# Differential attention with both maps' scores on row halves of the array, and a reordered neighbourhood attention

## What is computed

```python
def diff_attention(q, k, v, lam):            # q (B,Sq,H,2,d): 4 heads, two maps of d = 64
    s = einsum('bqhmd,bkhmd->bhmqk', qb, k) * scale
    p = softmax(s, axis=-1)
    a = p[:, :, 0] - lam * p[:, :, 1]
    return einsum('bhqk,bkhe->bqhe', a, v)
# latent queries: 512 own keys (with rotary) and 128 cached keys; prompt queries: 128 own keys
y_diff = rms_norm(y_diff, subln_g) * (1 - lam_init)

# neighbourhood attention, 8 heads of 64: softmax over an 8 x 16 window of the grid
# (with a relative bias) and the 128 cached keys; prompt queries: plain softmax
```

## Time and profile before

| | us |
|---|---|
| runs before | 2065.28, 2064.86, 2063.15 (median 2064.86) |
| the profiled execution's own time | 2058.49 |
| its span in the trace | 2056.4 |
| PE busy | 1963.3 (95% of the span) |
| DVE busy | 955.7 (46%) |
| ACT busy | 647.1 (31%) |
| POOL busy | 593.6 (29%) |
| differential stages | 236 to 456 and 1248 to 1451 |
| neighbourhood stages | 478 to 712 and 1473 to 1706 |

### The profile page before, as it was taken

How to read it: one execution, slowest core, us unless ns; L and a number is a source line. 1 busy time by engine, 2 the same in 40 slices (tenths; PEclk the granted TensorE clock), 3 DMA queues, 4 the chain that set the end, 5 groups by cost and what they waited for, 6 DMA issues and landing times.

```text
span 2056.4 us, 30590 instructions
## 1 busy us (share of the span) xinstructions
PE 1963.3 (95%) x12384; PEld 1782.0 (87%) x12384; DVE 955.7 (46%) x1480; ACT 647.1 (31%) x1101; POOL 593.6 (29%) x278
## 2 busy tenths in 40 slices
PE   6799989999999999999999999999999999999998
PEld 3698877889898999999878988888988899999996
DVE  5798666453444463421352143445344555443022
ACT  4323233323343321221352233333243332223121
POOL 2434311213222232233333332222322223313331
PEclk9999999999999999999999999999999999999999
DMA  7444320112121131122322221111221113212231
GB/s 294 151 158 145 127 101 31 42 52 93 61 64 52 62 102 62 52 72 81 125 101 94 88 72 62 42 42 42 83 72 62 57 58 99 66 51 72 72 111 74
DMA packets 50955, 172.13 MB, mean 84 GB/s; under 512 B 6656, under 2 KB 7296, under 8 KB 50816
## 3 DMA queue, kind: packets, MB, share of 16 engines
q1 hardware_dynamic: 41024, 146.60, 21.0%
q10 hardware_dynamic: 9792, 23.58, 3.3%
HBM read 162.82 MB, written 7.34 MB: 83 GB/s over the span
## 4 chain that ended last, share of the span: by engine, by line
PE 78%; DVE 14%; issue 4%; ACT 2%; DMA 1%; POOL 0%; SPq 0%; ACTq 0%; DVEq 0%; POOLq 0%
PE ps L1614 53%; PE ps L1502 4%; PE ps L1504 4%; PE ps L1503 4%; DVE mixed L1057 4%; PE ps L1688 3%; PE ps L1707 2%; PE ps L1726 1%; PE ps L1716 1%; DVE Pm L1328 1%; DVE nmax L1286 1%; ACT Pm L977 1%; DMA stage<-in_w_mod 1%; PE ps L1679 1%; PE ps L1689 1%
## 5 line engine op out<-in xcount | busy, mean ns | idle before, releaser
L728 POOL TENSOR_TENSOR wlo<-raw,whi 128x1024 fp32r<-128x1024 f32 x224 | 563.3, 2515 | 1319.7 <-ACT whi L786 1317.6
L1614 PE MATMUL ps<-bufB,whi 128*128 128x320 f32 x2816 | 541.8, 315 | 6.5 <-DVE vn L1183 4.0
L1614 PE MATMUL ps<-bufA,whi 128*128 128x320 f32 x2816 | 540.7, 314 | 4.9 <-DVE z L1448 1.4
L1614 PEld LDWEIGHTS ps<-bufB,whi 128*128 128x128 f32 x2816 | 443.5, 190 | 16.5 <-issue 11.5
L1614 PEld LDWEIGHTS ps<-bufA,whi 128*128 128x128 f32 x2816 | 442.3, 189 | 14.9 <-issue 10.1
L1614 PE MATMUL ps<-bufB,wlo 128*128 128x320 f32 x1408 | 323.4, 311 | 0.0
L1614 PE MATMUL ps<-bufA,wlo 128*128 128x320 f32 x1408 | 323.2, 311 | 0.0
L786 ACT ACTIVATE whi<-raw 128x1024 fp32r<-128x1024 f32 x224 | 237.6, 1061 | 210.5 <-PE ps L1614 125.0
L1614 PEld LDWEIGHTS ps<-bufB,wlo 128*128 128x128 f32 x1408 | 237.7, 190 | 0.0
L1614 PEld LDWEIGHTS ps<-bufA,wlo 128*128 128x128 f32 x1408 | 237.5, 189 | 0.0
L977 ACT ACTIVATE Pm<-ps,nmax 128x640 f32<-128x640 f32 (+2 forms) x160 | 100.0, 625 | 364.8 <-DVE nmax L1286 339.7
(11 more groups left out here) (217 smaller groups left out, 1898.6 us busy)
## 6 DMA issues: line engine op xcount, KB each, us to landing
raw<-in_wstream SPq DMA_DIRECT2D x224, 512.0 KB, 3.3
stage<-in_wstream SPq DMA_DIRECT2D x32, 512.0 KB, 4.5
stage<-in_w_mod SPq DMA_DIRECT2D x16, 512.0 KB, 15.2
out_y_sample<-X ACTq DMA_DIRECT2D x8, 512.0 KB, 2.7
Pm<-in_rpb ACTq DMA_DIRECT2D x12, 256.0 KB, 2.8
X<-in_x_sample SPq DMA_DIRECT2D x4, 512.0 KB, 10.9
xres<-in_x_sample ACTq DMA_DIRECT2D x4, 512.0 KB, 5.8
xres<-out_y_sample ACTq DMA_DIRECT2D x4, 512.0 KB, 5.9
```

The source lines that it names most:

```text
L728: pool.tensor_tensor(wlo[:, s % SPLITS, :], raw[:, s % RAWS, :], whi[:, s % SPLITS, :].bitcast(F32), ALU.subtract).then_inc(sems["lo"], 1)
L1614: ins = pe.matmul(ps[:, 2 * b + n, 0:HALF], wt[:, cols], src[:, part, base + k, n * HALF:(n + 1) * HALF], start=k == 0 and wt is hi and pa ...
```

## The change

In the differential stage one `S` step now makes both maps. The 512 own keys go in two halves of 256; for each half, map 0 is multiplied on rows 0 to 63 and map 1 on rows 64 to 127, into banks 4 and 5. The 128 cached keys of both maps go to a free quarter of banks 6 and 7, behind a wait for the copy and the value eviction of earlier units; ACT copies them to `Pm` at once. DVE takes the maximum of both maps' own keys in one instruction, of the cached keys in a second, and the smaller of the negated maxima in a third. A new step `EX` holds the exponentials: two for own keys, then two for cached keys (in place in `Pm`, with sums in `ectx`). PE's next `S` waits only for the first two. A new step `CB` adds the sums and combines the maps; it stands behind PV(u-1) in the order, so behind the value eviction on DVE. `TP`'s copy becomes two instructions (banks 6 and 7, 384 and 256 columns). `NR` moves from behind PV to behind the next `S`.

The new order for unit u is: S(u), NR, two parts, TP(u-1), EX(u), one part, PV(u-1), CB(u), YT.

In the neighbourhood stage TP(u-2) goes ahead of S(u), NM(u) ahead of the second place for parts, and YN behind that place.

```diff
@@ -94,13 +94,15 @@
...
-    ("S", "diff", False, 0): {"expd": 1, "nmax": 1, "sready": 1},
-    ("S", "diff", False, 1): {"chain": 1, "comb": 1, "expd": 1, "nmax": 1, "sready": 1, "stat": 1},
+    ("S", "diff", False, 0): {"copied": 1, "nmax": 3, "sready": 2},
+    ("EX", "diff", False): {"expd": 2},
+    ("CB", "diff", False): {"chain": 1, "comb": 1, "stat": 2},
...
 def differential():
     units = [(f, 0, t) for f in range(4) for t in range(TILES)]
-    out, late = [], []
+    out, late, norm = [], [], []
     for u, (f, hh, t) in enumerate(units):
-        out.append(("S", "diff", u, f, hh, t, 0))
-        out.append(None)
+        out += [("S", "diff", u, f, hh, t, 0)] + norm + [None]
+        norm = []
         if u:
             out.append(("TP", "diff", u - 1, *units[u - 1]))
-        out += [("S", "diff", u, f, hh, t, 1), None]
+        out += [("EX", "diff", u, f, hh, t), None]
         if u:
             out.append(("PV", "diff", u - 1, *units[u - 1]))
-        out += late
+        out += [("CB", "diff", u, f, hh, t)] + late
         late = []
         if f and t < 3:
-            out.append(("NR", "diff", f - 1, t))
+            norm = [("NR", "diff", f - 1, t)]
         if f and t == 3:
             late = [("YT", "diff", f - 1)]
     u = len(units) - 1
@@ -232,13 +234,12 @@
         f, _, t = units[u]
         if t == 4 and f < 3:
             out += [("E", 2 * f + 2), ("E", 2 * f + 3)]
-        out += [s + (0,) for s in both("S", u)]
         if u:
             out += both("TP", u - 2)
-        out.append(None)
+        out += [s + (0,) for s in both("S", u)] + [None]
         if u:
             out += both("PV", u - 2)[:1]
-        out += late + [None, ("NM", u)]
+        out += [("NM", u), None] + late
         late = []
         if u and units[u - 2][0] != f:
             late = [("YN", f - 1)]
...
     for n, step in enumerate(rest):
         s.append(step)
-        if step[0] == "S" and step[6] and n < before:
+        if step[0] == "S" and n < before:
             s += some(1)
...
-        scores = ps[:, 4:6, :].rearrange("p a c -> p (a c)")
-        turned = ps[:, 6:8, :].rearrange("p a c -> p (a c)")
-        out_pv = ps[:, 7, P:2 * P]
+        scores = ps[:, 4:6, :]
+        turned = ps[:, 6:8, 0:3 * P]
+        turned_at = [(6, 0), (6, P), (6, 2 * P), (7, 0), (7, P)]
+        ctx_scores = ps[:, 6:8, 3 * P:4 * P]
+        out_pv = ps[:, 7, 2 * P:3 * P]
...
-                            n = P if t == 4 else NTOK
-                            dst, src = Pm[:, slot, 0:n], scores[:, 0:n]
+                            if u >= 2:
+
+                                act_e.wait_ge(sems["tpready"], count.step("tpready", PLAN.unit["TP", name, u - 2]))
+                            if t < 4:
+                                act_e.wait_ge(sems["sready"], count.step("sready"))
+                                act_e.activation(Pm[:, slot:slot + 2, DEC:NTOK], ctx_scores, ACT.Copy).then_inc(sems["copied"], 1)
+                                act_e.wait_ge(sems["copied"], count.own("copied"))
+                            continue
...
+                    elif kind == "EX":
+                        _, name, u, f, hh, t = step
+                        slot, n = 2 * u % 4, P if t == 4 else DEC
+                        if u >= 2:
+                            act_e.wait_ge(sems["tpready"], count.step("tpready", PLAN.unit["TP", name, u - 2]))
+                        act_e.wait_ge(sems["nmax"], count.step("nmax", PLAN.unit["S", name, u]))
+                        for h in range(2):
+                            ins = act_e.activation(Pm[:, slot + h, 0:n], scores[:, h, 0:n], ACT.Exp,
+                                                   bias=nmax[:, slot + h:slot + h + 1], accum_out=esum[:, slot + h:slot + h + 1])
+                        ins.then_inc(sems["expd"], 1)
+                        act_e.wait_ge(sems["expd"], count.own("expd"))
+                        if t < 4:
+                            for h in range(2):
+                                ins = act_e.activation(Pm[:, slot + h, DEC:NTOK], Pm[:, slot + h, DEC:NTOK], ACT.Exp,
+                                                       bias=nmax[:, slot + h:slot + h + 1], accum_out=ectx[:, slot + h:slot + h + 1])
+                            ins.then_inc(sems["expd"], 1)
+                            act_e.wait_ge(sems["expd"], count.own("expd"))
...
-                        dst = AT[:, u % 2, 0:n] if name == "diff" else turned_sb[:, u % 2, 0:n]
-                        act_e.activation(dst, src, ACT.Copy).then_inc(sems["atready"], 1)
+                        if name == "na":
+                            act_e.activation(turned_sb[:, u % 2, 0:n], ps[:, 6 + u % 2, 0:n], ACT.Copy).then_inc(sems["atready"], 1)
+                        elif t == 4:
+                            act_e.activation(AT[:, u % 2, 0:P], turned[:, 0, 0:P], ACT.Copy).then_inc(sems["atready"], 1)
+                        else:
+                            act_e.activation(AT[:, u % 2, 0:3 * P], turned[:, 0, :], ACT.Copy)
+                            act_e.activation(AT[:, u % 2, 3 * P:NTOK], turned[:, 1, 0:2 * P], ACT.Copy).then_inc(sems["atready"], 1)
...
+                            slot, n = 2 * u % 4, P if t == 4 else DEC
+                            pair = slice(slot, slot + 2)
+                            dve.wait_ge(sems["sready"], count.step("sready", k=1))
+                            part = nmax[:, pair] if t == 4 else nparts[:, 0, :]
+                            dve.tensor_reduce(part, scores[:, :, 0:n], AX_X, ALU.max, negate=True).then_inc(sems["nmax"], 1)
+                            dve.wait_ge(sems["nmax"], count.own("nmax"))
+                            if t < 4:
+                                dve.wait_ge(sems["copied"], count.step("copied"))
+                                dve.tensor_reduce(nparts[:, 1, :], Pm[:, pair, DEC:NTOK], AX_X, ALU.max, negate=True).then_inc(sems["nmax"], 1)
+                                dve.wait_ge(sems["nmax"], count.own("nmax"))
+                                dve.tensor_tensor(nmax[:, pair], nparts[:, 0, :], nparts[:, 1, :], ALU.min).then_inc(sems["nmax"], 1)
+                                dve.wait_ge(sems["nmax"], count.own("nmax"))
+                            continue
...
-                        if m == 1:
-                            n, slot, r = P if t == 4 else NTOK, 2 * u % 4, u % 4 * 2
-                            dve.wait_ge(sems["expd"], count.step("expd"))
-                            dve.reciprocal(rsum[:, r:r + 2], esum[:, slot:slot + 2]).then_inc(sems["stat"], 1)
+                    elif kind == "CB":
+                        _, name, u, f, hh, t = step
+                        slot, r = 2 * u % 4, u % 4 * 2
+                        pair = slice(slot, slot + 2)
+                        dve.wait_ge(sems["expd"], count.step("expd", PLAN.unit["EX", name, u]))
+                        if t < 4:
+                            dve.tensor_tensor(esum[:, pair], esum[:, pair], ectx[:, pair], ALU.add).then_inc(sems["stat"], 1)
                             dve.wait_ge(sems["stat"], count.own("stat"))
-                            if True:
-
-                                dve.scalar_tensor_tensor(comb_c[:, 0:1], rsum[:, r + 1:r + 2], lam[:, layer, 6:7],
-                                                         esum[:, slot:slot + 1], ALU.mult, ALU.mult).then_inc(sems["chain"], 1)
-                                dve.wait_ge(sems["chain"], count.own("chain"))
-                                dve.scalar_tensor_tensor(Pm[:, slot, 0:n], Pm[:, slot + 1, 0:n], comb_c[:, 0:1],
-                                                         Pm[:, slot, 0:n], ALU.mult, ALU.add).then_inc(sems["comb"], 1)
-                                dve.wait_ge(sems["comb"], count.own("comb"))
+                        dve.reciprocal(rsum[:, r:r + 2], esum[:, pair]).then_inc(sems["stat"], 1)
+                        dve.wait_ge(sems["stat"], count.own("stat"))
+                        n = P if t == 4 else NTOK
+                        dve.scalar_tensor_tensor(comb_c[:, 0:1], rsum[:, r + 1:r + 2], lam[:, layer, 6:7],
+                                                 esum[:, slot:slot + 1], ALU.mult, ALU.mult).then_inc(sems["chain"], 1)
+                        dve.wait_ge(sems["chain"], count.own("chain"))
+                        dve.scalar_tensor_tensor(Pm[:, slot, 0:n], Pm[:, slot + 1, 0:n], comb_c[:, 0:1],
+                                                 Pm[:, slot, 0:n], ALU.mult, ALU.add).then_inc(sems["comb"], 1)
+                        dve.wait_ge(sems["comb"], count.own("comb"))
...
-                        pe.wait_ge(sems["expd"], count.before("expd"))
+                        if name == "diff" and u:
+                            pe.wait_ge(sems["expd"], count.step("expd", PLAN.unit["EX", name, u - 1], 1))
+                        else:
+                            pe.wait_ge(sems["expd"], count.before("expd"))
...
```

(24 more changed lines are left out.)

29 lines of the change are left out of this document (11 added, 18 removed).

## The result

| | before | after |
|---|---|---|
| runs, us | 2062.01 to 2065.28, median 2064.01 | 1981.20 to 1982.85, median 1982.37 |
| the profiled execution's own time, us | 2058.49 | 1982.85 |
| its span, us | 2056.4 | 1980.9 |

The ratio is 0.9605 with a 95% interval of 0.959 to 0.962: 82 us, 4.0% faster.

The account below looks back on a forecast made before the run. TensorE bounds the kernel: its own work, idle places and low-clock stretches. Scores -44, new stalls +11.5, old stalls -15, neighbourhood -14, clock -8: say -70 us from 2064.9, so 1995 us; range 1977 to 2030.

Parts of the forecast that it names:

- Score work: Differential stage, TensorE: pairing both maps' score matmuls on two row halves saves 41.0 us in latent and 3.4 in prompt units.
- the rival without overlap: Differential scores: pairs don't overlap when four matmuls stand in a row; 31 us of saving lost, 2026 us; chance 0.04.
- The chain of the unit: Differential stage: ScalarE's copies and exponentials before the next scores just fit, 0.2 us spare; 0.1 us a unit, 3 in all.
- The rival by which the exponentials bound the unit: Differential stage: ScalarE's chain exceeds TensorE's 3.7 us by 1 us, 34 us more, 2029 us; chance 0.18.
- The Trainium skill's warning on the evacuation of PSUM: Differential stage: tiling speeds up TensorE but not PSUM evacuation, which may become the bottleneck; cited for the 2029 us rival.
- old waits: Differential stages: TensorE's waits where NR or DM held VectorE before the maximum or the eviction go, -15 us.
- new ones: Differential stages: new TensorE stalls from the new chain and order, 3 + 4 + 2.5 + 2 = +11.5 us.
- the cached pair behind the eviction: Differential stage: cached-key scores wait for PV(u-2)'s eviction where a gate's tanh queues behind EX, once per layer, 2 us each.
- where DM and NR meet: Differential stage, three units of layer 0: VectorE isn't free for the eviction before the cached pair, about 0.8 us each.
- VectorE's three maximum instructions are off the path: Differential stage: the maxima end some 5 us after S(u) starts, while ScalarE asks for them at 6.6 us.
- The neighbourhood's order: Neighbourhood stage: NM ahead of the second place for parts and YN behind it remove TensorE's waits, -14 us.
- The clock: Both kinds of stage: fewer stretches at clock 0.50 behind TensorE's idle times, -8 us, ends 0 and -12.

## Why the prediction was right, and what it missed

**Score work: right.** Forecast -44 us; the sums by kind give 45.1 + 44.0 - 23.4 - 22.9 = 42.8 us. The 0.97 and 0.31 us of a unit, worked out from the neighbourhood's pairs, came to the hundredth, and the rival without overlap is refuted by the unit on one row half (1.83 us). The Trainium skill's rule weighed in the forecast, that weight loads overlap matmuls in flight only when the row group differs (TensorE: Matmul & The Clock Gate, Part 3: Packing small matmuls), doesn't hold in these traces either: the later groups of a half start with no gap in the changed kernel, and with both maps on one row half, where no other half is busy, matmuls still start every 0.215 us.

**Transposes: missed.** The forecast priced the row half from the first score instruction on, and took entering as paid inside it. Part of it lies in front, in the spacing of the instruction before. The old kernel entered a row half twice a unit, once right behind TP, and the new one once: TP's spacing fell from 11.8 and 11.3 to 7.9 and 7.8 us, 7.4 us in all. The two kernels with the extra matmul put the price at 0.25 us for once in and out. In the neighbourhood stage TP now stands in front of the scores, and there the spacing grew by 1.8 + 2.2 us, of which the cached scores gave back 1.0. Net -4.4 us that no step of the forecast had.

**The chain of the unit: right in kind, too tight in size.** The forecast had 0.2 us to spare and took 0.1 us a unit as a loss. Measured: 0.39 us to spare and no loss in ordinary units. The pieces: copies from 0.82 us behind TP's start, as said; an exponential with its sum takes (1309.17 - 1307.72) / 2 = 0.73 us, not 0.8. The rival by which the exponentials bound the unit is out: ScalarE is busy 94 of 207 us. The Trainium skill's warning on the evacuation of PSUM (TensorEngine Tiling (Array Packing), PSUM Bottleneck) does not come true in this kernel's trace.

**Idle time: the sum within 3 us, by luck.** Forecast: -15 of old waits and +11.5 of new ones, -3.5 in all; measured -0.6, made up otherwise. The old ones in front of scores and transposes went, 16.7 us. The new ones there are 15.0 (about 1 us of either is the start of each layer's first scores, which didn't change): 4.4 of the cached pair behind the eviction, 3.0 of it at the gate's tanh (forecast 4, with the right unit named), 7.6 in front of the scores (forecast 3) and 3.0 in front of TP (1.4 where DM and NR meet, forecast 2.5 with others; 0.8 at each layer's end, forecast 2). The step that failed is "VectorE's three maximum instructions are off the path", which end at 5 us where they are needed at 6.6. It holds for an ordinary unit. It was not made for the unit with the prompt's short TP and PV, and it gave the small instructions 0.2 us, where a GpSimd pass stretches one to as much as 1.74. Of the 6.6 us of waits for the exponential, 3.1 go with the held minimum, 1.1 are the short cover alone, and 2.4 follow a held L1342 and YT. Layer 1 thus lost 3.3 us where layer 0 gained 3.9.

**The neighbourhood's order: right.** Forecast -14 us of idle time; the waits of TP fell from 7.5 and 7.6 to 1.4 and 1.0 us, and PV's 1.2 and 1.0 went: 14.9 us. Layer 0, to be held against the earlier trace rows:

```profile
L1768 PE MATMUL ps<-ident,Pm 128*128 128x128 f32 x104 | 14.7, 273 | 1.4 <-DVE Pm L1375 1.4
```

**The clock: right in sign, too small.** Forecast -8 us, at most -12. By the traces, the time at 0.50 in the four stages fell from 30.7 to 6.8 us, and dense work, which has as many instructions, got 11.9 us shorter. In the differential and neighbourhood stages two stretches are left, both where a layer's last unit is drained, behind the waits at 1369.16 (0.8 us) and 1371.22 (1.7 us) and their like in layer 0; they answer to the earlier trace rows.

```profile
408.30:411.70 3.40, 3.24 (x13) 2.83 (x12) 3.19 (x7) 0.08 (x1) 0.00 (x0) 0.51 0.00 0
1370.90:1374.30 3.40, 3.08 (x12) 3.09 (x13) 2.90 (x5) 0.26 (x1) 0.00 (x0) 0.50 0.00 0
```

The profiled execution of the kernel before had less of it than most: its mean clock is 0.984. In the 23 later runs of that kernel the mean clock lies between 0.979 and 0.984. The four shortest, 2056.2 to 2057.4 us, have 0.984 (so have two of 2060.6 and 2061.1), and all seven of 2062.6 us or more have 0.979 or 0.980. The changed kernel has 0.988 to 0.990. The forecast subtracted a saving read from one execution from the median of others; the median of those runs was 6.4 us longer, to go by the later ones because of the clock, and that went too. The neighbourhood's new order alone shows the same from the other side: its differential stage of layer 0 has the code of before and spent 27.3 us at the low clock, 10 more than in the profiled execution of before.

**The sum.** Scores -42.8, transposes and the places of the cached scores -4.4, idle time of the differential stages -0.6 and of the neighbourhood -14.9, clock -11.9, value matmuls -0.4: -75.0 us, against 75.5 between the spans. The other 6 to 7 us, up to the medians, have no trace of their own: the runs' mean clocks speak for the clock, and no run here shows it directly. Counted so, of the 12.6 us missed the clock is about 10 and the transposes 4; the waits of the differential stages took 3 back.
